# The modulation's products in the stick-breaking stage, with the weights as the stationary operand

## The reference, cut to what matters

```python
sh1, sc1, g1, sh2, sc2, g2 = jnp.split(
    (jax.nn.silu(c) @ ada_w[layer] + ada_b[layer])[:, None, :], ADA_CHUNKS, axis=-1)
csh1, csc1, cg1, csh2, csc2, cg2 = jnp.split(
    jax.nn.silu(c_ctx) @ ada_w[layer] + ada_b[layer], ADA_CHUNKS, axis=-1)
```

## Time and profile before

| | |
|---|---|
| median of 3 runs | 3683.35 us (3675.93 to 3684.28) |
| profiled execution | 3693.07 us, span 3691.6 us |
| TensorE busy | 3388.8 us, 92% of the span |
| VectorE busy | 2330.3 us, 63% |
| ScalarE busy | 1228.1 us, 33% |
| GpSimd busy | 748.8 us, 20% |
| mean granted clock of TensorE | 0.944 of full |

### The profile page before, as it was taken

The page is one execution under the profiler, slowest core; times in us unless marked ns, Lnnn a source line. Parts: engine busy times, 40 slices in busy tenths (PEclk is TensorE's granted clock), DMA queues, the critical chain, the costliest instruction groups (busy, mean ns, idle before and its releaser), DMA issues. The chain is left out here.

```text
span 3691.6 us, 44814 instructions
## 1 busy us (share of the span) xinstructions
PE 3388.8 (92%) x17156; PEld 2798.5 (76%) x17156; DVE 2330.3 (63%) x4524; ACT 1228.1 (33%) x2087; POOL 748.8 (20%) x703
## 2 busy tenths in 40 slices
PE   7999899999999999997988989678899999999778
PEld 5555446888866688885776868668899999999777
DVE  4773334646455565454553348998968878878776
ACT  2343223323323332233452223223433333333333
POOL 1001222000100030004000010106834444444331
PEclk9678999999999999998998989789999999999989
DMA  3002332223211122222111222324588888888773
GB/s 131 12 7 89 119 125 66 97 95 102 89 51 46 41 97 94 100 92 67 57 40 63 97 69 86 135 99 180 210 285 298 310 299 294 315 291 301 255 267 112
DMA packets 181765, 515.15 MB, mean 140 GB/s; under 512 B 14769, under 2 KB 75185, under 8 KB 174897
## 3 DMA queue, kind: packets, MB, share of 16 engines
q1 hardware_dynamic: 127840, 305.69, 24.9%
q0 software_dynamic: 40464, 160.45, 12.0%
q10 hardware_dynamic: 13248, 46.15, 3.2%
HBM read 477.10 MB, written 35.13 MB: 139 GB/s over the span
## 5 line engine op out<-in xcount | busy, mean ns | idle before, releaser
L222 PE MATMUL bank<-h_hi,w_hi 128*128 128x512 f32 (+1 forms) x2720 | 1045.4, 384 | 95.7 <-ACT w_hi L197 20.1
L222 PE MATMUL bank<-h_lo,w_hi 128*128 128x512 f32 (+1 forms) x2720 | 1027.2, 378 | 0.0
L203 DVE TENSOR_TENSOR w_lo<-w_raw,w_hi 128x1024 fp32r<-128x1024 f32 (+1 forms) x508 | 647.2, 1274 | 282.1 <-ACT w_hi L197 280.7
L197 ACT ACTIVATE w_hi<-w_raw 128x1024 fp32r<-128x1024 f32 (+1 forms) x508 | 545.0, 1074 | 524.4 <-PE bank L222 461.2
L222 PE MATMUL bank<-h_hi,w_lo 128*128 128x512 f32 (+1 forms) x2720 | 647.6, 376 | 30.4 <-DVE w_lo L203 29.8
L222 PEld LDWEIGHTS bank<-h_hi,w_hi 128*128 128x128 f32 x2720 | 529.6, 195 | 183.7 <-issue 46.9
L222 PEld LDWEIGHTS bank<-h_hi,w_lo 128*128 128x128 f32 x2720 | 501.7, 193 | 102.9 <-DVE w_lo L203 36.7
L222 PEld LDWEIGHTS bank<-h_lo,w_hi 128*128 128x128 f32 x2720 | 531.4, 195 | 63.6 <-issue 7.7
L222 PE MATMUL bank<-e_hi,w_hi 128*128 128x384 f32 x832 | 285.9, 344 | 35.0 <-DVE x L2258 25.3
L2101 POOL DMA_INDIRECT own_row<-in_u_rows,own_e x128 | 198.2, 1548 | 440.2 <-DVE own_g L1999 180.7
L222 PE MATMUL bank<-e_lo,w_hi 128*128 128x384 f32 x832 | 282.6, 340 | 0.0
(11 more groups left out here) (400 smaller groups left out, 4614.4 us busy)
## 6 DMA issues: line engine op xcount, KB each, us to landing
w_raw<-in_w SPq DMA_DIRECT2D x476, 512.0 KB
ada_w<-in_ada_w POOLq DMA_DIRECT2D x24, 1024.0 KB, 5.1
expert_weights<-G ACTq DMA_DIRECT2D x24, 1024.0 KB, 4.2
Gin<-expert_weights SPq DMA_DIRECT2D x16, 1536.0 KB, 14.8
w_raw<-in_w SPq DMA_DIRECT2D x32, 704.0 KB
hidden_ahead<-u_stage ACTq DMA_DIRECT2D x40, 192.0 KB, 1.8
ahead<-hidden_ahead SPq DMA_DIRECT2D x10, 768.0 KB, 6.8
na_bias<-in_bias ACTq DMA_DIRECT2D x4, 896.0 KB, 4.6
```

The lines of the kernel that those rows point to most:

```text
L197: sc.activation(w_hi[s][:, 0:n], w_raw[raw_slot[u]][:, 0:n], ACT.Copy).then_inc(*w_hi_made.next(u))
L203: ve.tensor_tensor(w_lo[s][:, 0:n], w_raw[raw_slot[u]][:, 0:n], w_hi[s][:, 0:n], ALU.subtract).then_inc(*w_lo_made.next(u))
L222: m = te.matmul(out, wt, moving, start=(not low and k == 0 and moving is hi), stop=(low and k == len(blocks) - 1))
```

## The change

The two operands of the modulation's products trade places. The weights (128 x 128) become the stationary operand and `silu` (128 x 2) the moving one, so that each sum comes out as a column on 128 partitions, where `mod` wants it. A turn has 16 products (2 groups of 128 columns by 8 blocks) in place of 8. The copy, the tile `ada_rows` and the turning products are gone, and `ada_add` waits for the products and reads them in place.

```diff
-        rows_of = sb(st, "ada_rows", [2, 256])
...
-            for c in range(KT):
-                m = te.matmul(x_bank[0:2, 0:256], silu[:, c, :], ada_w[k % 2][:, c, :], start=(c == 0), stop=(c == KT - 1))
+            for n in range(2):
+                for c in range(KT):
+                    m = te.matmul(x_bank[:, 2 * n:2 * n + 2], ada_w[k % 2][:, c, n * P:(n + 1) * P], silu[:, c, :], start=(c == 0), stop=(c == KT - 1))
             m.then_inc(*pe.next("ada", k))
 
-        def ada_turn(k):
-            te.wait_ge(*dve.at("ada rows", k))
-            for n in range(2):
-                m = te.matmul(x_bank[:, 256 + 2 * n:258 + 2 * n], rows_of[:, n * P:(n + 1) * P], ident[0:2, 0:2], start=True, stop=True)
-            m.then_inc(*pe.next("ada turned", k))
-
-        def ada_rows(k):
+        def ada_add(k):
             ve.wait_ge(*pe.at("ada", k))
-            ve.tensor_copy(rows_of[:, :], x_bank[0:2, 0:256]).then_inc(*dve.next("ada rows", k))
-
-        def ada_add(k):
-            ve.wait_ge(*pe.at("ada turned", k))
             bias = col("ada_b", 2 * k, 2).unsqueeze(2).to_broadcast([P, 2, 2])
-            ve.tensor_tensor(mod[:, 2 * k:2 * k + 2, :], x_bank[:, 256:260].rearrange("p (n c) -> p n c", c=2), bias, ALU.add).then_inc(*dve.next("mod", k))
+            ve.tensor_tensor(mod[:, 2 * k:2 * k + 2, :], x_bank[:, 0:4].rearrange("p (n c) -> p n c", c=2), bias, ALU.add).then_inc(*dve.next("mod", k))
...
                         ada_sums(a)
-                        ada_turn(a)
...
-                        ada_rows(a)
                         ada_add(a)
```

## The result

The changed kernel takes 3731.02 us (median of 4 runs, 3725.60 to 3733.19) where the kernel before takes 3682.67 (4 runs, 3675.93 to 3684.28). The ratio is 1.0133, 95% interval 1.0115 to 1.0150: slower by 48 us. The forecast was 3724, +41, in a range of 3690 to 3755.

The account below looks back on a forecast made before the run. TensorE was taken to bound the kernel: 25 us saved at the high clock and 66 us lost to low clock gave +41 on the 3683.35 us median, so 3724 us, range 3690 to 3755.

Parts of the forecast that it names:

- What bounds the kernel: Modulation stage, 325 to 585 us: TensorE sets the pace, so changes to its time reach the kernel's end.
- The price at the high level: Modulation turns at high clock: single 4.65 to 3.57 us, first of a double slot 5.06 to 4.06; 25 us less.
- its own 0.111 us: Assumed time per new pass at the high clock, taken between 0.10 and 0.117 us; 32 passes a turn.
- the prediction's 1.67 us: Cost of one low-clock stretch: 16 passes of L954 take 5.28 us instead of 3.61.
- The clock: In each of 16 modulation slots TensorE's clock falls during or shortly after the turn; about 0.75 instead of 0.97.
- The step that rested on one place in the trace: At L447 to L451, 20 passes of 128x128 loads with one moving column had not raised the low clock.
- The size of the loss at the low level: Low clock in the modulation stage costs 66 us: 2.5 us per single slot, 5.8 per double slot, eight of each.
- The sum: Whole kernel: 25 us gained at the high clock against 66 lost at the low one, +41 us.
- What was hidden: Earlier L203 subtraction has nobody waiting; the ada_w fetch has some 6.5 us spare, of which the change takes at most 3.
- The first, a clock that holds: Rival: loads count as work for the clock once high, so 25 us faster, 3658 us; chance 0.12.
- The second (short falls only): Rival: one low stretch per slot, dense work restoring the clock at once, +2 us, 3685; chance 0.05.
- The third's upper bound: Rival: modulation stage low nearly throughout, or loads overlapping less, +80 us, 3763 us; chance 0.08.

Follow-up runs that it names:

- e1: Changed kernel with silu's two columns repeated 64 times, 128 moving columns a pass instead of 2; 3659.79 us, ratio 0.9907 to the kernel before.
- e6: Kernel before with the copy and turning products left out, last addition reading other numbers, so not computing mod; 3656.75 us, ratio 0.9926.
- e4: Changed kernel with silu padded to 128 moving columns by 126 columns of zeros; 3653.74 us, ratio 0.9905 to the kernel before.
- e7: e1 with each turn's 16 products done twice, at 128 moving columns; 3740.38 us, ratio 1.0152 to the kernel before.
- e5: Changed kernel, two moving columns, each step's first turn cut in four between L222 product groups where these stand ahead; 3710.26 us, ratio 1.0074 to the kernel before.
- e2: Changed kernel with silu's two columns repeated to 64 moving columns a pass; 3676.41 us, ratio 0.9976 to the kernel before.
- e8: Changed kernel, 2 moving columns, with each turn's 16 products done twice; 3887.06 us, ratio 1.0547 to the kernel before.

## Why the prediction was right, point by point

**What bounds the kernel.** Right. The stage's 45.9 us arrive at the end (48 by the medians), and its 29.8 us less in e1 arrive too (31).

**The price at the high level.** Right, and the gain a little low. A single turn of e1 holds TensorE for 336.75 - 333.25 = 3.50 us (3.57 forecast), the first of a double slot for 348.52 - 344.44 = 4.08 (4.06 forecast). From 4.65 and 5.06 that is 16 x 1.15 + 8 x 0.98 = 26.2 us. The forecast has 25; by its own 0.111 us, 32 passes are 3.55 and not 3.57, which makes it 26 too. The stage of e1 is 253.6 - 223.8 = 29.8 us shorter than that of the kernel before. Most of the 3.6 us between 26.2 and 29.8 can be read from the granted clock. The kernel before has four low stretches at the ends of pairs, from 379.1, 447.4, 515.7 and 570.3 us, and falls once more just before the stage ends, 14.5 low us in all. e1 has two and the last fall, 8.4 low us:

```profile
436.20:439.40 3.20, 3.20 (x16) 3.20 (x17) 2.43 (x4) 0.60 (x1) 1.28 (x2) 0.50 0.01 3
497.60:500.80 3.20, 3.06 (x15) 3.06 (x16) 2.67 (x5) 0.60 (x1) 1.33 (x3) 0.50 0.03 5
```

Two low stretches fewer, at the prediction's 1.67 us each, are an estimated 3.3 us. The prediction left these stretches out of its sum. Whether e1 has fewer because its turns are shorter or by where its pauses fall was not tested; e6 has two as well, e4 three. On the load, the pace of the passes and the Trainium skill (TensorE: Matmul & The Clock Gate, LDWEIGHTS) agree within a few per cent: its 0.107 us for 128 columns stands beside 3.49 / 32 = 0.109 in the changed kernel at the high level and 0.1125 by e7.

**The clock.** Right, and shown. The step that rested on one place in the trace was that loads with hardly a column behind them don't hold the clock. The place was weak: behind those loads TensorE stands idle from 1706.9 to 1710.8, so that the clock is low at 1710.8 says nothing of the loads, and only the 3.9 us of the loads themselves count. No row had shown a high clock falling in such a run. The kernel after shows it: high from 332.6 to 339.4 us, low from 339.6, with TensorE at work throughout the first stretch and for 13.05 of 13.4 us of the second. e1 to e4 change the columns alone and the clock goes with them, e5 changes only where the passes stand. What these runs can't part is the number of moving columns from the share of time in which columns move; the two go together in e1 to e4. The Trainium skill states the gate as one on how busy TensorE has been (same page, part 1), and its advice is to avoid idle gaps. Here matmuls and loads are both in flight for 6.70 of 6.70 us from 342.2 and the clock is at 0.50: for a load-heavy stream that advice is not enough, and the measurement decides.

**The size of the loss at the low level.** The total is 299.5 - 223.8 = 75.7 us, where the forecast had 66. Its parts were shared out wrongly. The forecast put 256 passes at the low level, the second turns of the double slots, 26 us. In the trace 459 of the 768 loads take over 250 ns, so 459 x 0.102 = 47 us: the last pair's turns are low but for one, and of the first turns of the eight double slots seven have low loads, from 6 of 32 to all of them. What is left, 29 us, is by subtraction the dense products behind the slots, where the forecast had 24 low stretches, 40 us. Of the eight single slots, which the forecast counted without low loads, four have no low load (402.7, 438.4, 477.9 and 550.6 us), three have 3 or 4 of 32, and the one in the last pair at 580.3 us has all of them. The two errors, +21 and -11, leave +10.

**The sum.** -29.8 + 75.7 = +45.9 against -25 + 66 = +41. The direction and the mechanism are shown; that the total is so close is in part luck, since misses of +21, -11 and -5 us leave +5.

**What was hidden.** Right. VectorE waits 110.6 us for the products in front of `mod` in the profile after, so it is still not what TensorE waits for; the last fetch is issued at 587.4 and its turn begins at 604.0; no new wait stands on TensorE. Its waits from 320 to 625 us:

```profile
PE bank L567 <- DVE sb_vT L363: 7.3, 3, 2.4
PE bank L954 <- DVE mod L960: 2.8, 8, 0.3
```

**The rivals.** The first, a clock that holds, is what e1 makes true by other means. Its 3658 us looks right for e1 (3659.79 measured), but on that chip the kernel before takes 8 us more: the gain is 31 us and not the rival's 25. The second (short falls only) fails at the stretches of 13.4 and 61.2 us. The third's upper bound, +80, was not reached, because the first three pairs do bring the clock back; in the last pair, from 554.5 us on, it is as this rival says.

## What to carry to other kernels

Cost a TensorE edit at both clock levels, and ask what the edit does to the columns that move, not to how busy the engine is: a swap of operands that makes a product all load and no columns can slow down the work behind it as well as itself. Where such products are wanted, make the moving operand wide enough to fill the time of the next load, by repeating or padding it; that took nothing here and turned 48 us lost into 31 gained, while half that width (e2) left some low stretches. If it can't be widened, put it between products that do move columns; that held the clock where it was done (e5). The gain itself comes from the copy and the turning products that are gone (e6), not from the swap's own passes.

## What the runs showed of the hardware that was not expected

With 128 moving columns, 126 of them zeros, the clock is as high as with data (0.97 and 0.97 from 325 to 585 us). And the code ahead of the stage, the same but for one clearing of a tile in e4, ended up to 15 us apart in the ten profiled runs. The granted clock from 90 to 300 us goes with it: at 0.65 the stage begins at 333.3 us (e1), at 0.68 at 331.1 (before and e8), at 0.71 at 327.5 and 327.7 (e2 and e6), and at 0.72 to 0.74 between 318.4 and 322.8 (the other five). What sets that clock was not tested.
